# Norms over the width in a two-block transformer kernel: logarithm read from the sums' bank, mean beside the exponential

## The reference

```
def rmsnorm(x, g):
    xf = x.astype(jnp.float32)
    y = xf * lax.rsqrt(jnp.mean(xf * xf, axis=-1, keepdims=True) + RMS_EPS)
    return (y * g.astype(jnp.float32)).astype(x.dtype)

# first block, for each of 2 layers
h = rmsnorm(x, g_mix_pre[l])
...                                   # gated delta net, sparse attention, HGRN2 on h @ w_in
mix = jnp.concatenate([o_a, o_b, o_c], axis=-1) @ w_out[l]
x = x + rmsnorm(mix, g_mix_post[l])
h = rmsnorm(x, g_ffn_pre[l])
x = x + rmsnorm(conv_geglu_ffn(h, ffn_w_up[l], ffn_conv[l], ffn_w_down[l]), g_ffn_post[l])

# second block, for each of 2 layers
x = x + 0.5 * gate(0) * _swiglu(norm_mod(x, 0), w_ffn_up[l, 0], w_ffn_down[l, 0])
x = x + gate(1) * _mixer(norm_mod(x, 1), ...)   # three branches, each normed over its own width
x = x + 0.5 * gate(2) * _swiglu(norm_mod(x, 2), w_ffn_up[l, 1], w_ffn_down[l, 1])
```

## Time and profile before

| | us |
|---|---|
| median of 3 runs | 3516.39 |
| lowest, highest | 3514.25, 3519.52 |
| the profiled execution | 3518.12 |
| its span, first to last instruction | 3516.4 |
| PE busy | 3493.3 (99%) |
| DVE busy | 1985.0 (56%) |
| ACT busy | 1493.8 (42%) |
| POOL busy | 54.1 (2%) |
| DMA, mean over the span | 105 GB/s |
| mean granted PE clock | 0.998 |

### The profile page before, as it was taken

How to read it: one execution, slowest core, us unless ns; L and a number is a source line. 1 busy time by engine, 2 the same in 40 slices (tenths; PEclk the granted TensorE clock), 3 DMA queues, 4 the chain that set the end, 5 groups by cost and what they waited for, 6 DMA issues and landing times.

```text
span 3516.4 us, 49823 instructions
## 1 busy us (share of the span) xinstructions
PE 3493.3 (99%) x20685; PEld 2944.9 (84%) x20685; DVE 1985.0 (56%) x3343; ACT 1493.8 (42%) x2392; POOL 54.1 (2%) x138
## 2 busy tenths in 40 slices
PE   9999999999999999999999999999999999999999
PEld 7888988887888888888888779888888888788888
DVE  6976677558875777454445566444533336663332
ACT  6466433335555533232223784222332226843221
POOL 0000000000000000000000000000000000000000
PEclk9999999999999999999999999999999999999999
DMA  3211244442202344434443212444332332213232
GB/s 129 70 44 52 81 151 151 152 139 82 67 26 67 120 144 149 158 101 150 150 148 122 84 55 69 154 144 154 127 103 99 93 91 80 66 37 102 96 102 84
DMA packets 110800, 368.72 MB, mean 105 GB/s; under 512 B 16240, under 2 KB 18672, under 8 KB 110576
## 3 DMA queue, kind: packets, MB, share of 16 engines
q1 hardware_dynamic: 110576, 365.54, 31.5%
HBM read 360.78 MB, written 4.19 MB: 104 GB/s over the span
## 4 chain that ended last, share of the span: by engine, by line
PE 91%; ACT 4%; DVE 4%; issue 1%; DMA 0%; POOL 0%; SPq 0%; ACTq 0%; DVEq 0%
PE bank L175 89%; ACT L400 1%; PE bank L259 1%; ACT tmp L190 1%; PE bank L181 1%; DVE wl L193 1%; ACT wh L190 1%; DVE score L217 1%; DVE ast L214 0%; DVE tmp L196 0%; ACT lr L190 0%; ACT ssh L190 0%; DVE ki L202 0%; DMA x<-in_x_dram 0%; DVE dv L196 0%
## 5 line engine op out<-in xcount | busy, mean ns | idle before, releaser
L175 PE MATMUL bank<-hh,wh 128*128 128x512 f32 (+2 forms) x3424 | 1279.5, 374 | 4.3 <-DVE hl L193 2.5
L175 PE MATMUL bank<-hh,wl 128*128 128x512 f32 (+2 forms) x3424 | 1282.0, 374 | 0.7 <-DVE wl L193 0.7
L175 PE MATMUL bank<-hl,wh 128*128 128x512 f32 (+2 forms) x3424 | 1278.1, 373 | 0.0
L190 ACT ACTIVATE wh<-raw 128x1024 fp32r<-128x1024 f32 (+1 forms) x542 | 558.9, 1036 | 1433.4 <-PE bank L175 1425.7
L193 DVE TENSOR_TENSOR wl<-raw,wh 128x1024 fp32r<-128x1024 f32 (+1 forms) x542 | 646.5, 1196 | 786.2 <-ACT wh L190 785.3
L175 PEld LDWEIGHTS bank<-hh,wh 128*128 128x128 f32 (+1 forms) x3424 | 645.0, 188 | 123.2 <-issue 12.9
L175 PEld LDWEIGHTS bank<-hh,wl 128*128 128x128 f32 (+1 forms) x3424 | 644.9, 188 | 115.5 <-issue 7.0
L175 PEld LDWEIGHTS bank<-hl,wh 128*128 128x128 f32 (+1 forms) x3424 | 645.1, 188 | 111.6 <-issue 6.1
L175 PE MATMUL bank<-ah,wl 128*128 128x512 f32 (+1 forms) x1188 | 436.1, 367 | 0.0
L175 PE MATMUL bank<-ah,wh 128*128 128x512 f32 (+1 forms) x1188 | 435.5, 367 | 0.0
L175 PE MATMUL bank<-al,wh 128*128 128x512 f32 (+1 forms) x1188 | 434.8, 366 | 0.0
(11 more groups left out here) (354 smaller groups left out, 3424.7 us busy)
## 6 DMA issues: line engine op xcount, KB each, us to landing
raw<-in_up_dram SPq DMA_DIRECT2D x264, 512.0 KB, 3.3
raw<-in_ada_dram SPq DMA_DIRECT2D x144, 512.0 KB, 4.3
raw<-in_in_dram SPq DMA_DIRECT2D x88, 512.0 KB, 3.3
raw<-in_down_dram SPq DMA_DIRECT2D x96, 448.0 KB, 3.3
raw<-in_down_dram SPq DMA_DIRECT2D x48, 512.0 KB, 3.6
raw<-in_out_dram SPq DMA_DIRECT2D x32, 512.0 KB, 3.3
x<-in_x_dram SPq DMA_DIRECT2D x16, 256.0 KB, 4.8
raw<-in_in2v_dram SPq DMA_DIRECT2D x8, 512.0 KB, 3.5
```

Of the source, the lines that this page charges most:

```text
L175: s = self.put(lambda e: e.matmul(out, lhsT, rhs, **kw), records * max(records * n, 2 * m) / 2.4)
L190: return self.put(lambda e: e.activation(out, x, func, **kw), cost, tables)
```

## The change

In `rstd` the logarithm now reads the bank with the sums itself: scale 1/n and the bias epsilon, taken from a column of the tile `eps`, are applied by the activation. DVE's mean, which the Newton step still needs, waits for the logarithm and no longer for the sums, and the Newton step's second instruction waits for the mean as well. The bank is free after the mean, as before. In `run`, more parts of the program get a section name; the tables of leads and ways are not changed.

```diff
@@ -1031,16 +1031,16 @@
     a, z = blocks[0], blocks[-1] + 1
     u, r, y = (stat.ap[:, 4 * i + a:4 * i + z] for i in range(3))
-    q.dve.wait_ge(b.done, stat.free)
+    q.act.wait_ge(b.done, stat.free, mem.eps_set)
+    s = q.act.activation(r, b.ap[:, a:z], ACT.Ln, bias=mem.eps[:, 0:1], scale=1.0 / n).then_inc(q.act.sem, 1)
+    q.dve.wait_ge(s)
     mean = q.dve.tensor_scalar(u, b.ap[:, a:z], 1.0 / n, EPS, ALU.mult, ALU.add).then_inc(q.dve.sem, 1)
     b.free = [mean]
-    q.act.wait_ge(mean)
-    s = q.act.activation(r, u, ACT.Ln).then_inc(q.act.sem, 1)
     q.act.wait_ge(s)
     s = q.act.activation(r, r, ACT.Exp, scale=-0.5).then_inc(q.act.sem, 1)
     q.dve.wait_ge(s)
     s = q.dve.tensor_tensor(y, r, r, ALU.mult).then_inc(q.dve.sem, 1)
-    q.dve.wait_ge(s)
+    q.dve.wait_ge(s, mean)
     s = q.dve.scalar_tensor_tensor(y, y, -0.5, u, ALU.mult, ALU.mult).then_inc(q.dve.sem, 1)
@@ -1470,11 +1470,12 @@
+    mem.program.section = "start", 0
     start(mem)
     for l in range(DEPTH):
         mem.program.section = "first", l
         mixer1(mem, l)
-        mem.program.section = None
+        mem.program.section = "ffn", l
@@ -1486,13 +1487,14 @@
             ready = mem.mod_ready[l][j]
+            if j != 1:
+                mem.program.section = "swiglu", 2 * l + j // 2
             normed(mem, lambda i: mem.dmod[:, l, 2 * j, i:i + 1], lambda i: mem.mod[:, l, 24 * j + i:24 * j + i + 1],
                         ready)
             if j == 1:
                 mem.program.section = "second", l
                 mixer2(mem, l, gate, ready)
-                mem.program.section = None
```

## The result

The changed kernel takes 3527.07 us (median of 8 runs, 3523.40 to 3531.43); the kernel before took 3517.62 beside it (8 runs, 3514.25 to 3519.82). The ratio is 1.0025, 95% interval 1.0016 to 1.0033: slower by some 9 us, where 0.5 us less was forecast, which can't be told from no change. The profiled execution has a span of 3524.5 us against 3516.4.

The account below looks back on a forecast made before the run. TensorE matmuls, busy for 99% of the span, were taken to bound the kernel. A gain of 1.7 us and a loss of 1.2 made -0.5, taking the 3516.4 median to 3515.9, said as 3516; range 3505 to 3530.

Parts of the forecast that it names:

- Price of the new logarithm: In every norm, the logarithm reading a bank with a bias column takes 263 ns instead of 202, 0.06 us more.
- Links on the path: At the start and stage ends, 14 norms no longer wait for the mean before the logarithm: 0.12 us each, 1.7 gained.
- Fillers: Matmuls of zeros at the joints should shrink with the shorter norm; if they didn't, the gain there is 0.
- The bank: At both first-block feed-forward ends, second-half sums wait for the first half's later mean in bank 5: 0.6 us lost each.
- the 1.2 of my sum: Total loss in us at the two first-block feed-forward ends from the mean freeing its bank later; bounds 0 and 2.5.
- The labels: New section names in the diff look up nothing in the tables of leads and ways: 0, no instruction changes.
- Table loads in the mixers: Rival, chance 0.32: mixers reordered worse, two more ACT table loads on the path in each of four, 10.3 us, giving 3526.
- The clock: Low PE clock at the second feed-forward end, 5.1 us recoverable, taken as a draw of +-3 us; part of a 0.20 rival.
- The rest of the sum: Whole kernel, apart from clock: 1.7 us gained by earlier logarithms and 1.2 lost by later means, -0.5 us.
- The signs I named: What traces would show: logarithms near 260 ns, mixer lengths, stretches at 0.50 clock; forecast wrong if mixers together move over 7 us.
- the slow rival: Mixers' order made anew and worse, by eight more ACT table loads: 10.3 us lost, 3526, chance 0.32.
- the fast case: Rival, chance 0.20: low-clock stretches go, all 34 norms gain, the later mean costs nothing: -9.2 us, 3507.

Follow-up runs that it names:

- e1: Kernel before with old waits and old order, only the logarithm reading the bank with scale and bias column: 3518.96 us against 3519.18, ratio 1.0002.
- e2: Kernel before in its old queue order, with the bank logarithm and the changed kernel's waits in 33 of 34 norms: 3525.45 us, ratio 1.0017.
- e6: New logarithm and waits in the second block's 16 norms alone, the rest as in the kernel before, planned anew: 3524.99 us, ratio 1.0016.
- e3: Changed kernel's queue order, but old waits and old logarithm in 33 of 34 norms: 3528.87 us, ratio 1.0027 to the kernel before.
- e11: Changed kernel, but the norms of the last mixer (second block's second layer) as before: 3524.85 us, ratio 1.0014 to the kernel before.
- e8: Kernel before, queues in their order, without the matmuls of zeros ahead of the second block: 3532.79 us, ratio 1.0036.
- e10: Changed kernel in its order, with 23 more matmuls of zeros, where its trace shows PE waiting: 3521.63 us, ratio 1.0008 to the kernel before.
- e5: New logarithm and waits in the start and first block alone (18 of 34 norms), rest as before, planned anew: 3524.99 us, ratio 1.0017.

## Why the prediction was wrong, step by step

*Price of the new logarithm: right.* 262 ns against 263 predicted, +0.06 us a link. The Trainium skill's page "ScalarE: Activation LUTs", section "What ACT_TABLE_LOAD costs", puts a pointer operand such as this bias at about 93 ns; the trace agrees, with the 89 of the earlier trace rows. Here the difference is 262 - 204 = 58, but between a logarithm from a bank and an exponential from SBUF, so that it doesn't price the bias alone. e1 shows that this price costs no measurable time.

*Links on the path: right size, wrong path.* A link does give what I said where its engines are free. In the first half's norm at the second swiglu end the Newton square starts at 2523.56 in before and 2530.37 in after, a shift of 6.81 where the products ahead of it are shifted by 6.95: 0.14 us gained, against 0.12. But PE doesn't wait for it, and the next long piece is shifted by 6.94 (2552.46, 2559.40). The same holds at the second mixer's end (7.7 at 1100.51 and 1108.20, 7.8 at 1179.98 and 1187.79), and the two later mixers take 270.7 and 271.1 us where they took 270.9 and 270.1. So of the 1.7 us nothing is to be seen at these ends. The second feed-forward end is 1.1 us shorter in spite of 3.4 us more at 0.50; how much of this are links and how much is order was not separated. Fillers shrank too, as forecast (the 115 that I gave for the earlier trace rows is the sum of the shapes listed there; the row itself counts 230). Tile zeros, after:

```profile
L259 PE MATMUL bank<-spinner,zeros x221: 220/396/794, 2.9 to 3178.3; 128*128 128x512 f32 x91, 128*128 128x256 f32 x8, 128*128 128x128 f32 x7, 128*128 128x384 f32 x5
```

*The bank: wrong place, right mechanism.* I read the means at 769.07 and 771.29 as two halves of one bank. By the order of the steps with their numbers they aren't: the first is the first half of the second norm, in bank 5, the other the second half of the first norm, in bank 7. The second half that uses bank 5 has its mean at 783.73, some 15 us later, and nothing waits there. The queueing exists: timeline of after, ACT and DVE.

```profile
771.30 1.22 DVE L193 TENSOR_TENSOR wl<-raw,wh 128x1024 fp32r<-128x1024 f32 x1 [2.16 <-ACT wh L190]
...
771.79 0.26 ACT L190 ACTIVATE stat<-bank,eps 128x2 f32<-128x2 f32 x1
...
772.23 0.26 ACT L190 ACTIVATE stat<-bank,eps 128x2 f32<-128x2 f32 x1
772.44 0.15 DVE L199 TENSOR_SCALAR stat<-bank 128x2 f32<-128x2 f32 x1
...
772.77 0.15 DVE L199 TENSOR_SCALAR stat<-bank 128x2 f32<-128x2 f32 x1
```

The first logarithm ends at 772.05, inside the split, and its mean stands behind it until 772.44, as I had worked out; that is 0.4 us, but PE's idle time at this end rose by no more than 0.07. Where nobody plans round the wait (e2) the two feed-forward ends do cost 0.9 and about 0.3 us (the latter an estimate: from 1186.88 to 1572.16 e2 is 1.35 us faster than before with 3.4 us less at 0.50, worth 1.7). That is the 1.2 of my sum, by luck: the way is DVE's split behind the waiting mean, which I had put at nothing ("DVE time, of which there is a lot"), and not sums that wait for a bank. And the first mixer's end, where I had no term, costs 1.1 more; for e2 as a whole, some 6 us, 1.2 was too small.

*The labels: right.* In e6, which has the new section names and the old norm in the first block, the pieces of that block have the numbers of instructions of before (154, 1620, 163, 1614).

*Table loads in the mixers: didn't happen.* The page of after:

```profile
L400 ACT ACT_TABLE_LOAD x112 | 143.7, 1283 | 2.0
```

Count, length and idle time are those of the earlier trace rows. The rival was right that the order is made anew and worse, and near in time (3526 against 3527.07), with a mechanism that isn't there. In the last mixer the place is another queue: DVE's. Timeline of after, DVE:

```profile
3076.26 0.15 DVE L199 TENSOR_SCALAR stat<-bank 128x4 f32<-128x4 f32 x1
3076.44 1.22 DVE L193 TENSOR_TENSOR wl<-raw,wh 128x1024 fp32r<-128x1024 f32 x1
3077.58 0.48 DVE L196 SCALAR_TENSOR_TENSOR fl<-bank,ftm,nfb 128x256 f32<-128x256 f32 x1
3077.98 0.27 DVE L211 TENSOR_REDUCE fst<-fl 128x1 f32<-128x128 f32 x1
```

And of before, where three splits stand ahead of all this and the next comes at 3072.96:

```profile
3066.77 3.49 DVE L193 TENSOR_TENSOR wl<-raw,wh 128x1024 fp32r<-128x1024 f32 x3
...
3070.48 0.15 DVE L199 TENSOR_SCALAR stat<-bank 128x4 f32<-128x4 f32 x1
3070.59 0.29 DVE L211 TENSOR_REDUCE fst<-fl 128x1 f32<-128x128 f32 x1
3070.79 0.47 DVE L196 SCALAR_TENSOR_TENSOR fl<-bank,ftm,nfb 128x256 f32<-128x256 f32 x1
```

The third of these splits, 1.22 us long, comes later in after and stands between the mean and the softmax steps. The shift between the kernels is 7.0 us at the start of this stretch and 7.7 at the fl step of 384 columns (3074.81 and 3082.53); about 1 us is left of it at the end of the mixer. That the mixer as a whole pays for the order is shown by e3 and e6 (+3.2 and +6.2 us there, by the chain's pieces as in the earlier trace rows) and e11 (within 0.1); that this one split is the cause is argued, not shown.

*The clock: the step that failed.* I took the low stretches as a symmetric draw of +-3 us around what the earlier trace rows shows, so that the sum had no term for them. They are a draw for one execution, but its mean belongs to the kernel, and the change moved it: 0.9977 to 0.9951. e8 and e10 show that the filling of the joints moves it, down and up, and time with it; e3 shows that the new order is enough, e5 that the first block is. So the sum missed 5 to 9 of the 9 us. The measured 3527.07 lies inside the range, whose upper end has 3.4 us for the clock, but on top of table loads that didn't happen.

*The rest of the sum: close by luck.* Take half of the 17.0 us more at 0.50 off the 8.1 us between the two spans, which is the most that they can have cost, and after is 0.4 us faster, against my 0.5. But no term is what I had made it: the links gave nothing at the ends named above, the bank cost nothing, the last mixer lost 1.0 where I had nothing, and the second feed-forward end gained.

*The signs I named.* "Mixers within 2 us of today would fell the slow rival; one that grows by over 3 us makes it": 402.8, 406.4, 270.7 and 271.1 us, so the second grew by 3.6 over the first layer's and by 3.2 over before's 403.2, though not for the rival's reason. Its stretch begins at 781.38 and holds the 10.24 us at 0.50; from 807.68 to 1187.79 the shift grows by 0.1 us only. A sign that counts microseconds without the clock could not tell the two apart. "More or fewer stretches at 0.50 clock" was the right thing to watch, and I had tied it to the fast case alone.

*Still open.* Which property of the new order empties the joints for the clock, given that PE's idle time there hardly rises (1.91 against 1.84 us); its one-column matmuls, idle times and pauses between lots were not separated. How often the low stretch comes at the first feed-forward end in either kernel: e1 has it with before's order. And whether the remedies of e10 and e11 add up.

## What to carry to other kernels

When PE is busy for 99% of the span and the rest are short joints, cost an edit in two currencies: the latency of the joint, and how well the array stays filled there, since the second can be worth more than the first; compare the mean granted clock over many runs, not the stretches of one trace. A step that is put behind another engine's step also goes behind everything in that engine's queue: look whether the planner sees the new wait, and which long weight copy is ahead of it. Before a wait in a bank is costed, the bank's number has to be read from the order of the steps, not guessed from the times.

## What the runs showed of the hardware that was not expected

PE's clock fell to 0.50 in joints where the longest wait of PE was 0.67 us (first feed-forward end of after, before 781.38) and 1.19 us (second, before 1538.9), and stayed there through stretches in which PE was busy all the time (783.05 to 793.29: busy 10.24 of 10.24 us). The Trainium skill's page "TensorE: Matmul & The Clock Gate", section "HAM oscillation — how this bites in real kernels", describes a clock that falls in waits for transfers of some microseconds. No wait of that length stands in these joints.

Matmuls whose result nobody uses are worth time here: without them before the second block 3532.79 us and clock 0.9920, with them 3519.07 and 0.9979 beside it. In the changed kernel two more behind every lot there cost 4.6 us (3531.64 against 3527.07), while 23 of them, most in seen waits, gave back 5.4.
